# A gated MLP's down projection in a two-block fp32 kernel, from 88 direct block products a layer to 77 by Strassen's scheme

## The chip, the cores and the metric

The kernel runs on one core of a Trainium2 chip. The metric is the device time of one execution in microseconds (us). TensorE (PE, with its weight loads shown apart as PEld) multiplies, VectorE (DVE), ScalarE (ACT) and GpSimd (POOL) work on elements, and the queue of SyncE (SPq) issues nearly all DMA transfers.

## The reference, cut to what matters

A first block (an RWKV branch beside latent attention) is followed by two layers of a second block. Everything is fp32, the sequence has 256 tokens and the model width is 1024. Each of the two layers ends in this, with `D_FF` = 2816:

```python
def conv_gated_mlp(x, w_up, conv_w, conv_b, w_down):
    h = x @ w_up
    hp = jnp.pad(h, ((0, 0), (CONV_WIDTH - 1, 0), (0, 0)))
    acc = conv_b
    for i in range(CONV_WIDTH):
        acc = acc + conv_w[i] * hp[:, i:i + seq]
    gate, val = jnp.split(acc, 2, axis=-1)
    return (jax.nn.gelu(gate) * val) @ w_down
...
        h = h + conv_gated_mlp(xn, w_up[layer], conv_w[layer], conv_b[layer], w_down[layer])
```

The change is about the last product, (256 x 2816) by (2816 x 1024), and the addition of its result to `h`.

## The kernel before

Each engine has one instruction stream, written by hand, and the streams meet at semaphores. The residual `h` is `xc[:, t, :]`, 128 tokens in each of t = 0, 1.

**Up projection.** It runs in 22 blocks m of 128 channels. TensorE fills one PSUM bank for a block (gate and value halves side by side, line 1343). VectorE then goes through a loop over m (lines 2758 to 2777): `scaled_rows(m + 1)` drains the next block's bank (line 2749), four multiply-adds apply the convolution (2767), three operations prepare the GELU (2771 to 2775), and `gate_part(m - 1)` (2755, 2757) writes `actT[:, m - 1, :]` after ScalarE's tanh. After the loop comes `gate_part(21)`. `actT[:, k, :]` holds 128 channels by 256 tokens, and the semaphore `act_T` counts these blocks. ScalarE's share for a block (lines 1869 and 1863) waits for `act_T` of two blocks before.

**Banks.** A pool "short" of six banks and a pool "long" of two are handed out in turn by `turn(key)`. `filling`, `when_full`, `emptying` and `when_empty` name the semaphores of a bank's current use.

**Weights.** A ring of four 2 MB slots is filled by SyncE's queue in the order of use, two transfers to a slot. A slot is filled again when the tile in it is released. `w_down` comes in six tiles `("down", l, n)`, of four blocks of 128 rows each (two in the last one).

**Down projection.** For each of the 22 blocks k, TensorE runs four products (line 1362), one for each of the quarters (t, j), j being a half of the 1024 columns, and each adds into its own bank over all k. One such fp32 product of 128x128 by 128x512 is two matmul instructions with a weight load each in the trace. VectorE adds the four banks into `xc` (line 2791), in the order (0,0), (1,0), (0,1), (1,1).

**Work of the next layer in that stretch.** Between `gate_part(21)` of layer 0 and those additions, VectorE runs what layer 1's state-space part needs: `state_steps` (from line 2294), `state_inputs` (from 2329), `state_sums` (from 2364), `state_maps` (2383, 2386) and two `sine_angles` (2392, 2394). The last operation of `state_steps` releases GpSimd's `raw_angles` (line 2838), one multiplication of 128x2048. Layer 1 has no such work behind it.

**End.** SyncE waits for all four additions of layer 1 and stores the whole output (1 MB) in one transfer (line 2963).

Of the kernel before, what the change touches and what calls it, by code (L numbers as in the profile page):

```python
# [15 lines left out]
P = 128  # L16
# [20 lines left out]
UP_TILES = FB // PAIRS  # L37
DOWN_K = 4
DOWN_TILES = -(-FB // DOWN_K)
RING_1, RING_2 = 3, 4  # L40
SLOT = KD * 512
TWO_PI = 2.0 * math.pi
# [70 lines left out]
def weight_tiles(w):  # L113
# [54 lines left out]
SCORES = [(0, (0, 1, 2, 3))] * 2 + [(1, (0, 1))] * 2 + [(1, (2, 3))] * 2  # L168
BLOCK = 32

SEMAPHORES = """a_bar_sc act_T cc_zero first_consts hT_even hT_odd ssq_ctx angle angle_raw b_spread a_made bk_ch block_T bonus_in c0 c_masked cv_made c_silu c_tanh consts crow d_bias d_hat
 d_rstd d_var d_w decays derived dt_exp e_made ends g_tanh gelu_in gelu_tanh h0 hp_pads k_tok kk_rn kk_sq kkf
 lam_exp lam_sum lora lw_in k_rate maps_used m_bias mix_gmlp mix_rw mix_ssm mod_cols off_made off_step out_done p2_load pads
 params_1 params_2 q_tok qk_rot qk_rstd qk_sum qk_taken qk_turned qk_var r_ch r_grown rk_used rotated rotated_used rstd_1 rstd_f rstd_lat scale_a scanned row_inv
# [4 lines left out]
def build(nc, w, consts, out):  # L179
# [16 lines left out]
    with ExitStack() as ctx:  # L196
# [210 lines left out]
        hp = take_work(M0 + 16128, 2, 2, 258)  # L407
        cv = take_work(M0 + 17160, 2, 2, SEQ)
        ge = take_work(M0 + 18184, 2, 2, SEQ)
        assert H0 + 2304 <= NW - (RING_2 - RING_1) * SLOT  # L410

        def shift_dest(key):
# [22 lines left out]
        def _(pe):  # L435
# [672 lines left out]
            for l in range(DEPTH):  # L1108
# [39 lines left out]
                            ins = tr(b[:, (2 * j + c) * P:(2 * j + c + 1) * P], bexp[:, j, c].rearrange("p a b -> p (a b)"), ident)  # L1148
                    ins.then_inc(*filling(("bT", l)))
                if l:  # L1150
                    to_channels("xa", xc, lambda j: when_empty(("down", l - 1, 2 + j)), small_maps)
                else:
                    to_channels("xa", xs2, lambda j: (S["z_f"], 2 * j + 2), small_maps)

# [178 lines left out]
                for n in range(UP_TILES):  # L1333
# [15 lines left out]
                pe.wait_ge(*turn(("down", l, 0)))  # L1349
                pe.wait_ge(*turn(("down", l, 1)))  # L1350
                pe.wait_ge(*turn(("down", l, 2)))
                pe.wait_ge(*turn(("down", l, 3)))
                acc = [bank_of(("down", l, 0)), bank_of(("down", l, 1)), bank_of(("down", l, 2)), bank_of(("down", l, 3))]
                for n in range(DOWN_TILES):
                    rows = min(DOWN_K, FB - n * DOWN_K)
                    wt = weights(("down", l, n), rows, 1024)
                    for q in range(rows):
                        k = DOWN_K * n + q
                        pe.wait_ge(S["act_T"], FB * l + k + 1)
                        for j in range(2):  # L1360
                            for t in range(2):
                                ins = mm(acc[2 * t + j][:, :], actT[:, k, P * t:P * t + P], wt[:, q, 512 * j:512 * j + 512],  # L1362
                                         start=(k == 0), stop=(k == FB - 1))
                                if k == FB - 1:
                                    ins.then_inc(*filling(("down", l, 2 * t + j)))
                    if n < DOWN_TILES - 1:
                        weights_done(ins=ins)
                    else:
                        weights_done(("down", l, 3))


        @block.scalar
        def _(act):
# [347 lines left out]
            for l in range(DEPTH):  # L1721
# [23 lines left out]
                if l:  # L1745
                    state_times(l)
                    state_parameters(l)
                    for q in range(4):
                        if q == 2:
                            channels_even(l, "xa", "attn_g", 0)  # L1750
                        square_sum(2 * l, q, when_empty(("down", l - 1, 2 * (q % 2) + q // 2)))
                channels_even(l, "xa", "attn_g", 2)
                take_maps()
                if l:
# [123 lines left out]
        def _(vec):  # L1878
# [640 lines left out]
            for l in range(DEPTH):  # L2519
# [231 lines left out]
                def gate_part(m):  # L2751

                    vec.wait_ge(S["gelu_tanh"], FB * l + m + 1)
                    p = m % 2
                    STT(out=ge[:, p, 1, :], in0=ge[:, p, 1, :], scalar=1.0, in1=cv[:, p, 0, :], op0=ADD, op1=MUL).then_inc(S["vec_step"], 1)
                    vec.wait_ge(S["vec_step"], next(vec_steps))
                    STT(out=actT[:, m, :], in0=ge[:, p, 1, :], scalar=0.5, in1=cv[:, p, 1, :], op0=MUL, op1=MUL).then_inc(S["act_T"], 1)  # L2757
                scaled_rows(0)
# [20 lines left out]
                if l + 1 < DEPTH:  # L2779
                    state_steps(l + 1)  # L2780
                    state_inputs(l + 1)
                    state_sums(l + 1)
                    state_maps(l + 1)
                    sine_angles(l + 1, 0)
                    sine_angles(l + 1, 1)
                for q in (0, 2, 1, 3):
                    t, j = q // 2, q % 2
                    vec.wait_ge(*when_full(("down", l, q)))
                    b = bank_of(("down", l, q))
                    x = xc[:, t, 512 * j:512 * j + 512]  # L2790
                    TT(x, x, b[:, :], ADD).then_inc(*emptying(("down", l, q)))  # L2791
                    vec.wait_ge(*when_empty(("down", l, q)))


        @block.gpsimd
# [85 lines left out]
        def _(sp):  # L2881
# [77 lines left out]
                        dst = dst.rearrange("p (k n) -> p k n", k=shape[0])  # L2959
                    sp.dma_start(dst, src).then_inc(slot_full[slot_of[n]], 16)  # L2960
            for q in range(4):
                sp.wait_ge(*when_empty(("down", DEPTH - 1, q)))
            sp.dma_start(out.rearrange("a (t p) d -> p (a t) d", p=P), xc[:, 0:2, :]).then_inc(S["out_done"], 16)
            sp.wait_ge(S["out_done"], 16)
# [20 lines left out]
```

## Time and profile before

| | us |
|---|---|
| median of three runs | 1183.38 (1181.89 to 1184.08) |
| span of the profiled execution | 1187.4 |
| down projection in the chain, layer 0, layer 1 | 75.53, 75.55 |
| up projection in the chain, layer 1 | 145.04 |
| last addition, then the store until it has landed | 0.69, 4.0 |

For the profiled execution the profile gives the span, from its first instruction to its last, and no other time of its own; the span is 4.0 us above the median of the runs. Times in rows are counted from the start of that span. A row of a timeline is: start, duration from the first to the last of the merged instructions, engine, line, operation, out<-in, shape, count, and in brackets the idle time before it with what ended it. The start-to-start distance of two neighbouring rows is often shorter than the duration of the first, because an engine starts the next instruction while the last one drains.

### The profile page before, as it was taken

The numbers are of one execution on the slowest core, as the hardware profiler recorded it, in microseconds if no ns is written. First come the engines' busy times: TensorE is split into PE (matmuls) and PEld (weight loads), VectorE is DVE, ScalarE is ACT, GpSimd is POOL, SyncE is SP. The second block draws the span as 40 slices with busy tenths as digits, with TensorE's granted clock in tenths as the row PEclk, the third lists the DMA queues.
The fourth block names the chain that finished last, engine by engine and source line by source line (L and its number), as shares of the span: only waits on it lengthen the run. The fifth ranks groups of instructions, "written<-read, shape, count | busy, mean of one in ns | idle before, by whom it ended". The sixth has DMA issues, their size and how long they took to land.

```text
span 1187.4 us, 15600 instructions
## 1 busy us (share of the span) xinstructions
PE 1136.4 (96%) x6191; PEld 793.8 (67%) x6191; DVE 645.7 (54%) x1360; ACT 336.6 (28%) x786; POOL 111.0 (9%) x107
## 2 busy tenths in 40 slices
PE   4899999989979999999999999999999999999998
PEld 2444857767878696555478888644555488888543
DVE  3222315688879944898226656631798135666400
ACT  2212213775633504325121121200525112112100
POOL 0000101210120011261000000100351000000000
PEclk9799999999888977999999999999999999999999
DMA  9722332000004211832248443424522354454410
GB/s 357 275 71 72 128 142 76 1 1 1 2 1 125 83 37 36 290 135 71 71 141 258 142 142 147 172 106 143 181 101 71 108 176 142 144 166 172 157 35 36
DMA packets 96666, 140.06 MB, mean 118 GB/s; under 512 B 12207, under 2 KB 63058, under 8 KB 96466
## 3 DMA queue, kind: packets, MB, share of 16 engines
q1 hardware_dynamic: 96228, 138.94, 34.3%
q8 instruction: 49, 0.80, 0.3%
q14 instruction: 23, 0.19, 0.1%
q10 hardware_dynamic: 366, 0.13, 0.0%
HBM read 138.01 MB, written 1.05 MB: 117 GB/s over the span
## 4 chain that ended last, share of the span: by engine, by line
PE 75%; DVE 18%; ACT 2%; issue 2%; DMA 2%; SPq 0%; POOL 0%; DVEq 0%; ACTq 0%
PE bank L1343 26%; PE bank L1362 13%; PE bank L826 12%; PE bank L480 2%; PE bank L473 2%; PE bank L1171 2%; DMA ring<-in_ada_w 2%; DVE work L2617 2%; DVE work L2612 1%; DVE ring L2175 1%; PE bank L619 1%; PE bank L1102 1%; PE bank L1161 1%; PE bank L812 1%; DVE rot L2597 1%
## 5 line engine op out<-in xcount | busy, mean ns | idle before, releaser
L1343 PE MATMUL bank<-work,ring 128*128 128x256 f32 x1024 | 222.7, 379 | 0.0
L1343 PEld LDWEIGHTS bank<-work,ring 128*128 128x128 f32 x1024 | 194.2, 190 | 26.2
L826 PE MATMUL bank<-work,ring 128*128 128x256 f32 (+1 forms) x432 | 141.1, 485 | 2.4 <-ACT work L1413 2.4
L1362 PE MATMUL bank<-ring,work 128*128 128x512 f32 x288 | 124.3, 592 | 0.0
L826 PEld LDWEIGHTS bank<-work,ring 128*128 128x128 f32 x432 | 82.8, 195 | 56.0 <-issue 49.4
L1869 ACT ACTIVATE work<-work,prm 128x256 f32<-128x256 f32 x88 | 48.0, 592 | 250.5 <-DVE work L2757 224.0
L1362 PEld LDWEIGHTS bank<-ring,work 128*128 128x128 f32 x288 | 54.7, 190 | 68.0 <-issue 67.4
L2749 DVE TENSOR_TENSOR work<-bank,turned 128x512 f32<-128x512 f32 x44 | 30.4, 692 | 112.0 <-PE bank L1343 111.9
L1343 PE MATMUL bank<-work 128*128 128x256 f32 x384 | 83.9, 379 | 0.0
L1343 PEld LDWEIGHTS bank<-work 128*128 128x128 f32 x384 | 73.0, 190 | 9.9
L2767 DVE SCALAR_TENSOR_TENSOR work<-work,prm 128x256 f32<-128x256 f32 x176 | 77.1, 480 | 4.2 <-ACT work L1869 2.6
L2802 POOL TENSOR_TENSOR small<-small,con 128x8 f32<-128x8 f32 (+4 forms) x23 | 32.6, 1418 | 429.6 <-DVE small L1987 123.2
L1171 PE MATMUL bank<-ring,work 128*128 128x512 f32 (+1 forms) x192 | 71.7, 526 | 0.0
L2791 DVE TENSOR_TENSOR xc<-xc,bank 128x512 f32<-128x512 f32 x8 | 5.5, 688 | 108.9 <-PE bank L1362 108.9
L1171 PEld LDWEIGHTS bank<-ring,work 128*128 128x128 f32 x192 | 35.7, 190 | 31.8 <-issue 30.3
L1967 DVE SCALAR_TENSOR_TENSOR work<-work,prm 128x512 f32<-128x512 f32 x10 | 7.5, 752 | 56.4 <-ACT work L1436 56.4
L2736 DVE TENSOR_TENSOR xc<-xc,bank 128x512 f32<-128x512 f32 x8 | 5.5, 688 | 46.9 <-PE bank L480 46.9
L1742 ACT ACTIVATE work<-xc 128x512 f32<-128x512 f32 x12 | 7.5, 629 | 78.8 <-DVE xc L2791 58.7
L480 PE MATMUL bank<-ring,mixT 128*128 128x512 f32 x64 | 27.9, 594 | 2.0 <-ACT mixT L1853 2.0
L1779 ACT ACTIVATE work<-work,small 128x64 f32<-128x64 f32 x64 | 16.2, 335 | 44.9 <-DVE work L2599 44.9
L1171 PE MATMUL bank<-work 128*128 128x512 f32 x64 | 28.7, 596 | 0.0
L2838 POOL TENSOR_TENSOR work<-small,con 128x2048 f32<-128x2048 f32 x2 | 7.3, 3654 | 225.3 <-DVE small L2319 163.9
(454 smaller groups left out, 1772.4 us busy)
## 6 DMA issues: line engine op xcount, KB each, us to landing
ring<-in_w_up SPq DMA_DIRECT2D x32, 1024.0 KB, 7.7
ring<-in_w_in SPq DMA_DIRECT2D x24, 1024.0 KB, 7.7
ring<-in_w_down SPq DMA_DIRECT2D x16, 1024.0 KB, 5.9
ring<-in_ada_w SPq DMA_DIRECT2D x12, 1024.0 KB, 11.0
work<-in_w_up SPq DMA_DIRECT2D x12, 1024.0 KB, 7.7
ring<-in_w_out SPq DMA_DIRECT2D x10, 1024.0 KB, 6.2
work<-in_w_in SPq DMA_DIRECT2D x4, 1024.0 KB, 8.5
work<-in_w_down SPq DMA_DIRECT2D x4, 1024.0 KB, 5.8
```

The costliest lines, as they stand in the source:

```text
L473: mm(b[:, :], mixT[:, k, P * t:P * t + P], out_weights[j][:, k, :], start=(k == ks[0]), stop=False)
L480: ins = mm(b[:, :], mixT[:, k, P * t:P * t + P], out_weights[j][:, k, :], start=False, stop=(k == ks[-1]))
L826: ins = mm(b[0:rows, 0:toks], wt[:, k, off:off + rows], hT[:, k, 0:toks], start=(k == 0), stop=(k == KD - 1))
L1171: ins = mm(b[:, 0:cols], xnT[:, k, P * t:P * t + P], wt[:, k, off:off + cols], start=(k == 0), stop=(k == KD - 1))
L1343: ins = mm(b[:, SEQ * half:SEQ * half + SEQ], wt[:, KD * half + k, P * j:P * j + P], xnT[:, k, :], start=(k == 0), stop=(k == KD - 1))
L1362: ins = mm(acc[2 * t + j][:, :], actT[:, k, P * t:P * t + P], wt[:, q, 512 * j:512 * j + 512], start=(k == 0), stop=(k == FB - 1))
L1779: ins = A.activation(qkr[:, c, t, 64 * h:64 * h + 64], rot_a[:, h, :], ACT.Copy, scale=small[:, 296 + 8 * i + h:297 + 8 * i + h])
L1869: ins = A.activation(cv[:, m % 2, half, :], hp[:, m % 2, half, 2:SEQ + 2], ACT.Identity, scale=k2(l, "conv2", 1, FB * half + m), bias=k2(l ...
L2617: ins = V.tensor_tensor_scan(gs[:, s % 2, SEQ * c:SEQ * c + SEQ], small[:, 440 + s:441 + s].to_broadcast([P, SEQ]), xr[:, SEQ * c:SEQ * c ...
L2749: TT(hp[:, p, :, 2:SEQ + 2], bank_of(("up", l, m))[:, :].rearrange("p (a n) -> p a n", a=2), rep(scale_row, 2), MUL).then_inc(*emptying((" ...
L2767: ins = STT(out=cv[:, p, half, :], in0=hp[:, p, half, tap:tap + SEQ], scalar=k2(l, "conv01", 1, 44 * tap + FB * half + m), in1=cv[:, p, ha ...
L2802: return G.tensor_tensor(out_, in_, C("negpow", 1, rows).to_broadcast([rows, n]), POW)
```

## The change

The 22 blocks of 128 rows are taken in 11 pairs. A pair with left blocks a(k, t) (k = the block of the pair, t = the tokens) and right blocks b(k, j) gives four quarters of the output. These come out of seven products instead of eight, and each of the seven adds into a bank of its own over all pairs: product 5 in a "long" bank, the other six in all six "short" banks. Seven left operands are needed for a pair, of which five are sums or differences (`row_sums`, for two pairs at once, five instructions over 2x128 elements), and seven right operands, of which five are sums or differences (`column_sums`, one pair at a time, five instructions of 128x512). VectorE forms all of them. The column sums have two buffers, by p % 2, so those of pair p wait until pair p - 2 is used. At the end, twelve additions or subtractions replace the four, in the order of the products 5, 1, 4, 7, 2, 3, 6. The last two pairs run interleaved, two products of the same number one after the other.

In VectorE's stream, `row_sums(0)` to `row_sums(4)` come at the ends of blocks m = 4, 8, 12, 16, 20, `column_sums(0)` and `(1)` at the ends of blocks 18 and 19, `row_sums(5)` and `column_sums(2)` after the loop, and `column_sums(3)` to `(7)` each behind one part of the next layer's state work. The output leaves in four transfers of 256 KB, each after the last addition to its quarter.

```diff
+DOWN_ORDER = (5, 1, 4, 7, 2, 3, 6)
+DOWN_LAST = (7, 2, 3, 6)
...
+                def down_product(i, p, last):
+                    wt, q = down_w[p // 2], 2 * (p % 2)
+                    one, two = actT[:, 2 * p, 0:P], actT[:, 2 * p + 1, P:2 * P]
+                    left = {1: row_sum[:, 0, p, :], 2: row_sum[:, 1, p, :], 3: one, 4: two, 5: row_sum[:, 2, p, :], 6: row_sum[:, 3, p, :], 7: row_sum[:, 4, p, :]}[i]
+                    cs = col_sum[p % 2]
+                    right = {1: cs[0], 2: wt[:, q, 0:512], 3: cs[1], 4: cs[2], 5: wt[:, q + 1, 512:1024], 6: cs[3], 7: cs[4]}[i]
+                    return mm(bank_of(("down", l, i))[:, :], left, right, start=(p == 0), stop=last)
...
+                for p in range(DOWN_PAIRS - 2):
+                    if p % 2 == 0:
+                        down_weights(p // 2)
+                    pe.wait_ge(S["row_sums"], 6 * l + p // 2 + 1)
+                    for i in DOWN_ORDER:
+                        if p == 0:
+                            pe.wait_ge(*turn(("down", l, i), "long" if i == 5 else "short"))
+                        if i == 1:
+                            pe.wait_ge(S["column_sums"], DOWN_PAIRS * l + p + 1)
+                        ins = down_product(i, p, False)
...
+                    ins.then_inc(S["pair_used"], 1)
+                down_weights(DOWN_TILES - 1)
+                pe.wait_ge(S["row_sums"], 6 * l + 6)
+                for i in DOWN_ORDER:
+                    if i == 1:
+                        pe.wait_ge(S["column_sums"], DOWN_PAIRS * (l + 1))
+                    ins = down_product(i, DOWN_PAIRS - 2, False)
...
+                    ins = down_product(i, DOWN_PAIRS - 1, True)
+                    ins.then_inc(*filling(("down", l, i)))
...
+                def column_sums(p):
+                    n, q = index[("down", l, p // 2)], 2 * (p % 2)
+                    vec.wait_ge(slot_full[slot_of[n]], 32 * fills[n])
+                    if p >= 2:
+                        vec.wait_ge(S["pair_used"], (DOWN_PAIRS - 2) * l + p - 1)
...
+                    TT(cs[0], b11, b22, ADD)
+                    TT(cs[2], b21, b11, SUB)
+                    TT(cs[4], b21, b22, ADD)
+                    TT(cs[1], b12, b22, SUB)
+                    TT(cs[3], b11, b12, ADD).then_inc(S["column_sums"], 1)
...
                     if m:
                         gate_part(m - 1)
+                    if m and m % 4 == 0:
+                        row_sums(m // 4 - 1)
+                    if m in (18, 19):
+                        column_sums(m - 18)
                 gate_part(FB - 1)
+                row_sums(5)
+                column_sums(2)
...
+                added(5, (0, 0, SUB), (0, 1, ADD))
+                added(1, (0, 0, ADD), (1, 1, ADD))
+                added(4, (0, 0, ADD), (1, 0, ADD))
+                added(7, None, (0, 0, ADD))
+                added(2, (1, 1, SUB), (1, 0, ADD))
+                added(3, (1, 1, ADD), (0, 1, ADD))
+                added(6, None, (1, 1, ADD))
```

`row_sums(n)` waits for `act_T` of its four blocks and then runs five instructions. An addition of `added` waits for the one before it. The left blocks `one` and `two` and the right blocks `wt[...]` are read where they lie, so products 2 and 5 need no column sum. The readers of `xc` behind layer 0 (transposes on TensorE, squares on ScalarE) now wait for the last addition to each quarter, `DOWN_LAST`.

## Rows read from the trace of the kernel before

**Rows 1.** The page's first line.

```profile
span 1187.4 us, 15600 instructions
```

**Rows 2.** The chain that ended last: start, us, what.

```profile
753.84 75.53 PE bank L1362 x176
...
1106.56 75.55 PE bank L1362 x176
...
1182.19 0.69 DVE xc L2791
```

**Rows 3.** The down products' line: ns min/median/max, first and last start.

```profile
L1362 PEld LDWEIGHTS bank<-ring,work x288: 190/190/190, 753.5 to 1181.1; 128*128 128x128 f32 x144
```

**Rows 4.** VectorE's timeline, layer 1, up blocks 18, 20 and 21.

```profile
1092.78 0.69 DVE L2749 TENSOR_TENSOR work<-bank,turned 128x512 f32<-128x512 f32 x1 [2.47 <-PE bank L1343]
...
1096.00 0.42 DVE L2775 TENSOR_TENSOR work<-work 128x256 f32<-128x256 f32 x1
1096.34 0.42 DVE L2755 SCALAR_TENSOR_TENSOR work<-work 128x256 f32<-128x256 f32 x1
1096.79 0.42 DVE L2757 SCALAR_TENSOR_TENSOR work<-work 128x256 f32<-128x256 f32 x1
...
1106.59 0.69 DVE L2749 TENSOR_TENSOR work<-bank,turned 128x512 f32<-128x512 f32 x1 [2.47 <-PE bank L1343]
...
1112.33 1.80 DVE L2767 SCALAR_TENSOR_TENSOR work<-work,prm 128x256 f32<-128x256 f32 x4 [1.30 <-ACT work L1869]
...
1116.54 0.42 DVE L2757 SCALAR_TENSOR_TENSOR work<-work 128x256 f32<-128x256 f32 x1
```

**Rows 5.** SyncE's queue: issues of down weights, layer 1.

```profile
1065.15 14.69 SPq L2960 DMA_DIRECT2D ring<-in_w_down  x4
```

**Rows 6.** VectorE's timeline, layer 0, the next layer's state work.

```profile
764.17 0.23 DVE L2294 TENSOR_SCALAR small<-small,con 128x8 f32<-128x8 f32 x1
...
769.10 1.93 DVE L2329 TENSOR_TENSOR small<-small 128x8 f32<-128x8 f32 x1 [1.79 <-ACT small L1675]
...
773.91 0.29 DVE L2364 TENSOR_TENSOR work<-small,work 128x128 f32<-128x128 f32 x1
...
775.87 1.39 DVE L2383 TENSOR_SCALAR work<-work,con 128x64 f32<-128x64 f32 x8
777.17 0.69 DVE L2386 TENSOR_TENSOR work<-work,con 128x512 f32<-128x512 f32 x1
777.77 0.69 DVE L2392 TENSOR_SCALAR work<-work 128x1024 f32<-128x1024 f32 x1
```

**Rows 7.** GpSimd's timeline in the same stretch.

```profile
767.39 3.62 POOL L2838 TENSOR_TENSOR work<-small,con 128x2048 f32<-128x2048 f32 x1 [163.86 <-DVE small L2319]
```

**Rows 8.** The timeline of all engines, layer 1's scans.

```profile
882.33 1.27 POOL L2867 TENSOR_TENSOR work<-work 128x512 f32<-128x512 f32 x1
882.37 1.78 DVE L2612 TENSOR_TENSOR work<-work 128x512 f32<-128x512 f32 x1
```

**Rows 9.** Windows: busy us of each engine, granted TensorE clock, DMA share, GB/s.

```profile
259.00:263.00 4.00, 1.08 (x7) 0.62 (x6) 3.80 (x9) 1.33 (x5) 0.00 (x0) 1.00 0.00 0
263.00:267.00 4.00, 4.00 (x27) 2.93 (x26) 3.65 (x13) 2.59 (x8) 0.00 (x0) 1.00 0.02 4
...
340.00:343.50 3.50, 0.10 (x1) 0.00 (x0) 3.38 (x5) 2.69 (x6) 1.93 (x3) 1.00 0.00 0
...
346.00:353.70 7.70, 7.70 (x50) 7.36 (x51) 2.67 (x5) 1.08 (x2) 0.72 (x2) 0.50 0.00 0
```

**Rows 10.** TensorE's timeline: the starts that ended those two stalls.

```profile
262.76 0.63 PE L568 MATMUL bank<-con,xc 128*128 128x128 f32 x4 [2.92 <-ACT xc L1630]
...
345.99 0.45 PE L661 MATMUL bank<-work,ring 128*128 128x64 f32 x1 [5.89 <-DVE ring L2048]
```

**Rows 11.** DMA issues: KB each, median us to landing.

```profile
out<-xc SPq DMA_DIRECT2D x1, 1024.0 KB, 4.0
...
work<-in_gmlp_w_s SPq DMA_DIRECT2D x2, 256.0 KB, 2.9
```

More of the change, by code:

```diff
@@ L409, in build @@
         ge = take_work(M0 + 18184, 2, 2, SEQ)
+        row_sum = take_work(M0 + 2048, 5, DOWN_PAIRS, P)
+        col_sum = ([mixT[:, 2 * i:2 * i + 2, :].rearrange("p a b -> p (a b)") for i in range(4)] + [rot_flat],
+                   [take_work(a, 512) for a in (M0 + 9088, M0 + 9600, G0 + 3072, G0 + 3584, G0 + 4096)])
         assert H0 + 2304 <= NW - (RING_2 - RING_1) * SLOT
@@ L1150, in _ @@
                 if l:
-                    to_channels("xa", xc, lambda j: when_empty(("down", l - 1, 2 + j)), small_maps)
+                    to_channels("xa", xc, lambda j: when_empty(("down", l - 1, DOWN_LAST[2 * j + 1])), small_maps)
                 else:
@@ L1348, in _ @@
                     weights_done(("up", l, m))
[L1349 to L1366, printed above, removed]
+                down_w = {}
@@ new lines, in down_weights @@
+                def down_weights(n):
+                    down_w[n] = weights(("down", l, n), min(DOWN_K, FB - n * DOWN_K), 1024)
+                for p in range(DOWN_PAIRS - 2):
[8 more added lines that the diff above has]
+                        ins = down_product(i, p, False)
+                        if i == 2 and p % 2:
+                            weights_done(ins=ins)
+                    ins.then_inc(S["pair_used"], 1)
@@ L1372, in _ @@
+                weights_done(("down", l, 2))
         @block.scalar
@@ L1750, in _ @@
                             channels_even(l, "xa", "attn_g", 0)
-                        square_sum(2 * l, q, when_empty(("down", l - 1, 2 * (q % 2) + q // 2)))
+                        square_sum(2 * l, q, when_empty(("down", l - 1, DOWN_LAST[q])))
                 channels_even(l, "xa", "attn_g", 2)
@@ L2757, in gate_part, with row_sums @@
                     STT(out=actT[:, m, :], in0=ge[:, p, 1, :], scalar=0.5, in1=cv[:, p, 1, :], op0=MUL, op1=MUL).then_inc(S["act_T"], 1)
+                def row_sums(n):
+                    first, last = 2 * n, min(2 * n + 2, DOWN_PAIRS)
+                    vec.wait_ge(S["act_T"], FB * l + 2 * last)
+                    a = actT[:, 2 * first:2 * last, :].rearrange("p (n k) (t c) -> p n k t c", k=2, t=2)
+                    a11, a12, a21, a22 = a[:, :, 0, 0], a[:, :, 1, 0], a[:, :, 0, 1], a[:, :, 1, 1]
+                    TT(row_sum[:, 0, first:last, :], a11, a22, ADD)
+                    TT(row_sum[:, 1, first:last, :], a21, a22, ADD)
+                    TT(row_sum[:, 2, first:last, :], a11, a12, ADD)
+                    TT(row_sum[:, 3, first:last, :], a21, a11, SUB)
+                    TT(row_sum[:, 4, first:last, :], a12, a22, SUB).then_inc(S["row_sums"], 1)
+                def column_sums(p):
[3 more added lines that the diff above has]
+                        vec.wait_ge(S["pair_used"], (DOWN_PAIRS - 2) * l + p - 1)
+                    wt = slot(n)[:, 1024 * q:1024 * q + 2048].rearrange("p (k j c) -> p k j c", k=2, j=2)
+                    b11, b12, b21, b22 = wt[:, 0, 0], wt[:, 0, 1], wt[:, 1, 0], wt[:, 1, 1]
+                    cs = col_sum[p % 2]
+                    TT(cs[0], b11, b22, ADD)
[3 more added lines that the diff above has]
+                    TT(cs[3], b11, b12, ADD).then_inc(S["column_sums"], 1)
                 scaled_rows(0)
@@ L2777, in _, with add_product, added @@
                         gate_part(m - 1)
+                    if m and m % 4 == 0:
+                        row_sums(m // 4 - 1)
+                    if m in (18, 19):
+                        column_sums(m - 18)
                 gate_part(FB - 1)
-                if l + 1 < DEPTH:
+                row_sums(5)
+                column_sums(2)
+                more = l + 1 < DEPTH
+                if more:
                     state_steps(l + 1)
+                column_sums(3)
+                if more:
                     state_inputs(l + 1)
+                column_sums(4)
+                if more:
                     state_sums(l + 1)
+                column_sums(5)
+                if more:
                     state_maps(l + 1)
+                column_sums(6)
+                if more:
                     sine_angles(l + 1, 0)
+                column_sums(7)
+                if more:
                     sine_angles(l + 1, 1)
[L2786 to L2789, printed above, removed]
+                for p in range(8, DOWN_PAIRS):
+                    column_sums(p)
+                def add_product(i, t, j, op):
                     x = xc[:, t, 512 * j:512 * j + 512]
-                    TT(x, x, b[:, :], ADD).then_inc(*emptying(("down", l, q)))
-                    vec.wait_ge(*when_empty(("down", l, q)))
+                    return TT(x, x, bank_of(("down", l, i))[:, :], op)
+                def added(i, one, two):
+                    vec.wait_ge(*when_full(("down", l, i)))
+                    if one:
+                        add_product(i, *one).then_inc(S["vec_step"], 1)
+                        vec.wait_ge(S["vec_step"], next(vec_steps))
+                    add_product(i, *two).then_inc(*emptying(("down", l, i)))
+                    vec.wait_ge(*when_empty(("down", l, i)))
+                added(5, (0, 0, SUB), (0, 1, ADD))
[5 more added lines that the diff above has]
+                added(6, None, (1, 1, ADD))
         @block.gpsimd
```

17 lines of the change are left out of this document (9 added, 8 removed).

## The prediction, made before the changed kernel was run

> **What bounds the kernel now.** I read the chain of waits first, since a saving counts only where it shortens that chain. In both layers the down projection is one unbroken piece of TensorE work, 75.53 and 75.55 us [rows 2], and in layer 1 only one addition and the store stand behind it. So TensorE is the bound here and a product less is time less. A layer has 88 products, each two of the 176 matmuls of that piece: 75.55 / 88 = 0.859 us a product. Then VectorE's timeline, since it gets new work: in the up projection it works 4.4 of every 6.9 us and then waits for TensorE (the bracket of 2.47 us [rows 4]); in the down projection it is free but for layer 0's state work [rows 6]. The question is whether that slack lies where the sums are needed.
>
> **What is removed.** 11 products a layer: 77 x 0.859 = 66.1 us against 75.55, so 9.4 us a layer, 18.9 in all, if TensorE never waits.
>
> **Prices of the sums.** An independent 128x512 addition in SBUF starts 0.60 us before the next instruction and lasts 0.69 (777.17 to 777.77 [rows 6]). So `column_sums` is 5 x 0.60 = 3.0 us of VectorE's time, with its signal 4 x 0.60 + 0.69 = 3.1 us after its start. At 128x256 the distance is 0.34 (1096.00 to 1096.34 [rows 4]), so `row_sums` is 5 x 0.34 = 1.7, with 0.1 for its wait on the last `act_T`. At 128x128 the row lasts 0.29 [rows 6]; by the 0.08 that two neighbours overlap, the distance is 0.21 and `row_sums(5)` 1.05. The upper bound is a start only after the end, as for dependent neighbours (0.45 for 128x256 [rows 4], so 0.73 at 512). I take the lower figure, because the five instructions don't depend on each other.
>
> **VectorE's walk into the down projection.** Let 0 be the start of the down piece in the chain (1106.56 in layer 1). The `row_sums` of blocks 4 to 16 take 1.8 us of a slack of 2.47: free. Block 18 begins at -13.78 and its body takes 4.35 (1092.78 to 1096.79, and 0.34 [rows 4]). Its weight tile was issued 41 us ahead [rows 5], so `column_sums(0)` doesn't wait: 3.0, done at -6.4. That is already later than the -6.9 at which block 19 wants to begin. Block 19 with `column_sums(1)`: 7.35, to +0.9. Block 20: 4.35 and `row_sums(4)` 1.8, to +7.1. Block 21 has no bank to drain; in the trace it takes 1112.33 to 1116.96 with both last gate parts [rows 4], so 4.6: +11.7. `row_sums(5)`: +12.8. `column_sums(2)`: signal at +15.9. The drain of bank 21 falls at about +1.6, ahead of product 6 of pair 0, which takes that bank at +5.2, so no bank is waited for.
>
> **Stall 1, both layers.** A pair takes 7 x 0.859 = 6.01 us. Pairs 0 and 1 have their sums, so TensorE has run them and product 5 of pair 2 at 2 x 6.01 + 0.86 = +12.9. Product 1 then waits until 15.9, and with a signal and a weight load that wasn't run ahead (0.19 [rows 3]) starts at 16.15. **3.3 us lost.** The wait is ahead of product 1, so everything of the pair but product 5 is queued behind it.
>
> **After that, layer 1.** The sums of pair p may start when pair p - 2 is used and are needed 6.01 + 0.86 us later; they take 3.3 with the signals. No stall up to pair 9.
>
> **Stall 2, both layers: the last two pairs.** They run interleaved, so product 1 of pair 9 comes after two products 5, and it waits for the sums of pair 10. Those share a buffer with pair 8 and start when its last product is done (0.2 after it on the array, a matmul being longer than its distance to the next). 0.2 + 3.1 + 0.25 = 3.55, less 2 x 0.86: **1.8 us lost** in each layer, on a VectorE that was idle before.
>
> **Layer 0: the state work between the sums.** `column_sums(2)` frees VectorE at 15.8. `state_steps` takes 3.1 (764.17 to its release of GpSimd just ahead of 767.39 [rows 6, 7]): 18.9. Then GpSimd multiplies for 3.6 us. The trace shows what a VectorE addition with two SBUF operands does meanwhile: 1.93 for eight elements, ended with GpSimd's instruction, and 1.78 in place of 0.69 for one of 128x512 that began behind a GpSimd one [rows 6, 8]. The port is taken for a whole instruction, and the other waits. `SBUF — State Buffer` of the Trainium skill, section "SBUF: two separate sides", calls this an exclusive lock taken by whoever starts first; the trace agrees, by the 1.78 us. Either GpSimd gets in after the first sum of pair 3 (signal at 25.7), or after the fifth (signal at 22.0, and `state_inputs` waits until 25.6). Both ways `state_inputs` (2.9, from 771.03 to 773.91 [rows 6]) ends near 28.6 and the sums of pair 4 near 31.7. Product 1 of pair 4 starts at 32.0; without any stall it would at 4 x 6.01 + 0.86 = 24.9. So **7.1 us are lost by pair 4**, the 3.3 of stall 1 among them. `state_sums` (773.91 to 775.87, 2.0), `state_maps` (1.9, to 777.77) and the sine angles (two of 1.9, by the same timeline) with 3.1 of sums each are under 6.01, so VectorE catches up, and it stays hidden. Cover is thin there: a part over 2.9 us would show.
>
> **The ends.** Twelve additions replace four. They come two to a product of number i, 2 x 0.73 against 1.72 us of two products, so they keep up; the last one is alone, 0.69 after the last matmul, as before [rows 2]. The readers behind layer 0 find the other quarters done earlier, and this one at the same distance: nothing. Store: 1 MB landed 4.0 us after its issue, a 256 KB transfer in 2.9 [rows 11], though a load. Quarters one to three leave while TensorE or VectorE works. Bounds: 0 (a fixed cost fills the 4.0) and 2.0; I take 1.4, a little over 4.0 - 2.9, because a load's 2.9 shares its queue with others.
>
> **The clock.** Until now TensorE was never idle in this piece. Does a stall of 3.3 us lower it to 1.2 from 2.4 GHz? After a stall of 2.92 the granted clock stayed at 1.00; in one of 5.89 us it fell 3.5 us after the engine stopped, and 7.7 us of work then ran at 0.50 [rows 9, 10]. The stalls here (3.0 to 3.8 us) lie between. Bounds: nothing, and half of 7.7 = 3.9 us a stall; that row's work was sparse, this one is dense. I take 1.5 us for the whole run, one short fall. `TensorE: Matmul & The Clock Gate` of the Trainium skill, section "Why this matters for your kernels", speaks against this change, since it wants no idle gap over about 3 us between bursts; by it every stall 1 would cost, by the 2.92 row none would. No row shows a dense stream with such a gap.
>
> **Sum.** Layer 0: 9.4 - 7.1 - 1.8 = +0.5. Layer 1: 9.4 - 3.3 - 1.8 = +4.3. Store +1.4, clock -1.5. Gain 4.7 us, some 12 of 18.9 given back to waits. The walk is made in the profiled execution, whose span is 1187.4 [rows 1]; the median is 4.0 lower, or 0.3%, which changes no term. 1183.4 - 4.7 = **1178.7 us**.
>
> **Rivals.**
> 1. *VectorE keeps up.* The stalls are nearly gone: 18.9 + 1.4 = 20, so 1163. For it: VectorE is idle for 45 us of each down piece. Against it: the 29.6 us of listed work between -13.8 and +12.9, where only 26.7 fit. Chance 0.08. A middle case, where layer 0's state work hides but stall 1 stays, gives 18.9 - 2 x 5.1 + 1.4 = 10, so 1173: 0.10.
> 2. *The sums cost 0.73 each* (slower side of the price). Column sums are 3.65, row sums 2.2. The same walk gives a signal for pair 2 at 18.7, stall 1 of 6, stall 2 of 2.4, and 10.5 by pair 4 in layer 0: 21.3 lost of 18.9, with the store 1.0 slower, 1184.4. It decides from about 0.70 a sum. Against it: 777.17 to 777.77. Chance 0.08.
> 3. *The clock falls and stays down, slower than before.* If each stall of 3 us or more (one in layer 1, two in layer 0) brings 7.7 us at half clock, it costs 3 x 3.9 = 11.6 and not 1.5: 1183.4 - 4.8 - 1.4 + 11.6 = 1188.8. It decides from 6.2 us of clock loss. For it: the fall 3.5 us into the one long stall. Against it: 2.92 without one, and work that is dense on both sides. By the page's sentence this would be the outcome. Chance 0.12.
>
> The forecast keeps 0.62, between 1176 and 1182.5. A measurement of this kernel tells about 0.2%, 1181.0 and 1185.7, from no change. Faster: the forecast's 0.55 below 1181.0, and 0.18 of rival 1: 0.73. Same: the forecast's upper 0.07, and most of rival 2: 0.14. Slower: 0.13. The range for 8 in 10 takes in the middle case and rival 2: 1172 to 1185.
>
> **What would show it.** TensorE's matmuls of the down line, in the profile of the changed kernel: 77 products a layer, at the old distance. In the table of waits, TensorE on VectorE's column sums: two long waits in layer 1 (about 3.1 and 1.6), three or four in layer 0, 12 to 14 us in all. VectorE's timeline: `column_sums(2)` ends 15.9 us after TensorE's first down product. GpSimd's 128x2048 lies inside or right behind the sums of pair 3. The pieces: 75.0 and 71.2 us, longer by what the clock takes. The windows behind each stall show a granted clock of 1.00, or 0.50. The prediction is wrong if a column sum takes under 2.6 or over 3.5 us, if the clock stays down for more than some 6 us, or if another wait (a bank, a weight tile) appears among the first three pairs.

## The result, and the profile after

The changed kernel took 1177.43 us (median of 20 executions, 1171.11 to 1189.57) against 1184.4 (20 executions, 1178.09 to 1192.37) for the kernel before on the same chips. The ratio is 0.9938, its 95% interval 0.9918 to 0.9959, which is 7.3 us less (4.9 to 9.7); the two medians are 7.0 apart. The execution of 1189.57 us is a slow one and is left out of the ratio. The prediction was 1178.7, or 4.7 less than its 1183.4. The profiled execution took 1176.57 us with a span of 1174.8.

The page's first line, and the down products in the line's own view (ns min/median/max, first and last start):

```profile
span 1174.8 us, 15721 instructions
```

```profile
L1364 PE MATMUL bank<-work x116: 592/592/697, 755.1 to 1170.1; 128*128 128x512 f32 x116
...
L1364 PE MATMUL bank<-mixT,work x96: 592/592/1222, 749.1 to 1170.9; 128*128 128x512 f32 x96
...
L1364 PE MATMUL bank<-ring,work x72: 592/592/1001, 748.2 to 1167.5; 128*128 128x512 f32 x72
...
L1364 PE MATMUL bank<-rot,work x24: 592/592/1061, 750.8 to 1165.8; 128*128 128x512 f32 x24
```

These are 308 matmuls, 2 x 77 products of two each, in place of 352. The chain that ended last (start, us, what) no longer has the down projection as one piece [rows 2]; each layer's is broken where a column sum ended the wait:

```profile
767.90 4.02 DVE work L2802
773.78 35.53 PE bank L1364 x82
812.56 10.57 PE bank L1364 x24
...
1116.23 41.48 PE bank L1364 x96
1160.96 10.58 PE bank L1364 x24
```

TensorE's timeline shows the same from the array's side. The first row of each layer is the start of the down projection, the brackets are its waits, the last row its last product:

```profile
748.21 1.02 PE L1364 MATMUL bank<-ring,work 128*128 128x512 f32 x2
...
764.30 3.78 PE L1364 MATMUL bank<-mixT,work 128*128 128x512 f32 x4 [3.05 <-DVE mixT L2805]
...
773.78 2.84 PE L1364 MATMUL bank<-work 128*128 128x512 f32 x6 [0.19 <-DVE work L2805]
...
779.89 1.94 PE L1364 MATMUL bank<-mixT,work 128*128 128x512 f32 x4
...
812.56 1.12 PE L1364 MATMUL bank<-work 128*128 128x512 f32 x2 [1.54 <-DVE mixT L2805]
...
822.11 1.02 PE L1364 MATMUL bank<-mixT,work 128*128 128x512 f32 x2
...
1100.15 1.02 PE L1364 MATMUL bank<-ring,work 128*128 128x512 f32 x2
...
1116.23 1.98 PE L1364 MATMUL bank<-mixT,work 128*128 128x512 f32 x4 [3.04 <-DVE mixT L2805]
...
1160.96 1.12 PE L1364 MATMUL bank<-work 128*128 128x512 f32 x2 [1.55 <-DVE mixT L2805]
...
1170.50 1.02 PE L1364 MATMUL bank<-mixT,work 128*128 128x512 f32 x2
```

VectorE's timeline and GpSimd's row, from which come the sums' prices, the blocked sum in layer 0, and the last addition:

```profile
763.56 0.69 DVE L2805 TENSOR_TENSOR mixT<-ring 128x512 f32<-128x512 f32 x1
...
767.22 0.69 DVE L2801 TENSOR_TENSOR work<-ring 128x512 f32<-128x512 f32 x1
767.82 4.10 DVE L2802 TENSOR_TENSOR work<-ring 128x512 f32<-128x512 f32 x1
...
773.05 0.68 DVE L2805 TENSOR_TENSOR work<-ring 128x512 f32<-128x512 f32 x1
...
1112.06 0.29 DVE L2787 TENSOR_TENSOR work<-work 128x128 f32<-128x128 f32 x1
...
1113.08 0.68 DVE L2801 TENSOR_TENSOR mixT<-ring 128x512 f32<-128x512 f32 x1
...
1115.49 0.69 DVE L2805 TENSOR_TENSOR mixT<-ring 128x512 f32<-128x512 f32 x1
...
1171.63 0.69 DVE L2856 TENSOR_TENSOR xc<-xc,bank 128x512 f32<-128x512 f32 x1 [0.31 <-PE bank L1364]
```

```profile
767.38 3.99 POOL L2917 TENSOR_TENSOR work<-small,con 128x2048 f32<-128x2048 f32 x1 [169.32 <-DVE small L2342]
```

The store among the DMA issues (KB each, median us to landing), which answers to [rows 11]:

```profile
out<-xc SPq DMA_DIRECT2D x4, 256.0 KB, 2.0
```

**Where the time went.** The spans differ by 12.6 us, but that isn't all the change's. In this profile layer 0's down projection begins at 748.2, in that of before at 753.7, both counted from a first matmul; in the seven experiments on the changed kernel that start lies anywhere from 743.0 to 753.2, though nothing ahead of the down projection's sums differs, and at 748.1 in the kernel before with another store. I count that stretch as chance. Between the two down projections both profiles take the same 277.19 us (829.37 to 1106.56 before, 823.13 to 1100.32 after). What is left is the change's own:

| piece, us | before | after | gained | predicted |
|---|---|---|---|---|
| down projection, layer 0 (748.38 to 823.13) | 75.53 | 74.75 | 0.8 | 0.5 |
| down projection, layer 1 (1100.32 to 1171.52) | 75.55 | 71.20 | 4.35 | 4.3 |
| last addition's start to the end of the span | 5.2 | 3.2 | 2.0 | 1.4 |
| clock, for the whole run (a fall in layer 0 cost nothing, see below) | | | 0 | -1.5 |
| sum | | | 7.2 | 4.7 |

The pieces are counted 0.17 us behind the first matmul, as the chain of before does. The sum of 7.2 agrees with the 7.3 of the timed runs.

### The profile page after: what moved, and what is told of

Same layout as the page of the kernel before. It is cut to its first block, busy times and chain, and to the rows that moved or that the text cites. A ratio compares the mean times of both kernels' runs of the same rounds, so it can differ in the third digit from the quotient of the medians.

```text
span 1174.8 us, 15721 instructions
## 1 busy us (share of the span) xinstructions
PE 1114.0 (95%) x6147; PEld 777.2 (66%) x6147; DVE 744.5 (63%) x1546; ACT 336.8 (29%) x786; POOL 111.4 (9%) x107
## 3 DMA queue, kind: packets, MB, share of 16 engines
HBM read 138.01 MB, written 1.05 MB: 118 GB/s over the span
## 4 chain that ended last, share of the span: by engine, by line
PE 69%; DVE 24%; issue 3%; ACT 2%; DMA 2%; SPq 0%; POOL 0%; DVEq 0%; ACTq 0%
PE bank L1349 24%; PE bank L832 12%; PE bank L1364 8%; PE bank L486 2%; PE bank L479 2%; PE bank L1177 2%; DMA ring<-in_ada_w 2%; DVE work L2640 2%; DVE work L2635 1%; DVE ring L2198 1%; PE bank L625 1%; PE bank L1108 1%; PE bank L1167 1%; DVE work L2815 1%; DVE rot L2620 1%
## 5 line engine op out<-in xcount | busy, mean ns | idle before, releaser
L1349 PEld LDWEIGHTS bank<-work 128*128 128x128 f32 x384 | 73.0, 190 | 9.9
L1364 PE MATMUL bank<-work 128*128 128x512 f32 x116 | 54.3, 595 | 3.3 <-DVE mixT L2805 3.1
L1177 PEld LDWEIGHTS bank<-ring,work 128*128 128x128 f32 x192 | 35.7, 190 | 31.8 <-issue 30.3
L1364 PE MATMUL bank<-mixT,work 128*128 128x512 f32 x96 | 47.8, 615 | 6.1 <-DVE mixT L2805 6.1
L1364 PEld LDWEIGHTS bank<-work 128*128 128x128 f32 x116 | 21.8, 190 | 32.1 <-issue 26.3
L1364 PEld LDWEIGHTS bank<-mixT,work 128*128 128x128 f32 x96 | 18.5, 195 | 30.7 <-issue 22.3
L1364 PE MATMUL bank<-ring,work 128*128 128x512 f32 x72 | 36.5, 598 | 0.0
L2759 DVE TENSOR_TENSOR xc<-xc,bank 128x512 f32<-128x512 f32 x8 | 5.5, 687 | 46.9 <-PE bank L486 46.9
```

What stands on the lines that cost most here:

```text
L1177: ins = mm(b[:, 0:cols], xnT[:, k, P * t:P * t + P], wt[:, k, off:off + cols], start=(k == 0), stop=(k == KD - 1))
L1349: ins = mm(b[:, SEQ * half:SEQ * half + SEQ], wt[:, KD * half + k, P * j:P * j + P], xnT[:, k, :], start=(k == 0), stop=(k == KD - 1))
L1364: return mm(bank_of(("down", l, i))[:, :], left, right, start=(p == 0), stop=last)
```

## The experiments

My theory is the prediction's walk: the 11 products are really saved, 9.4 us a layer, and what is lost again is lost at (a) stall 1, because `column_sums(2)` stands behind too much VectorE work, (b) stall 2, because pair 10 shares a buffer with pair 8, and (c) in layer 0, GpSimd's multiplication between the sums of pair 3. The rival is that the array doesn't run sums at the old rate, or that waits taken away come back as others (VectorE too slow, a clock fall behind each stall). "First to last start" below is the time from TensorE's first to its last matmul row in a down projection: 73.90 and 70.35 us in the changed kernel. In the version without waits it is 65.24. Ratios are to the kernel before on the same chip: 1185.28 us for the first four experiments, 1184.42 for the others. A single execution has no ratio, and its time says little, since the changed kernel's own executions lie between 1171 and 1190; there the trace carries the reading.

### One store

```diff
                 sp.wait_ge(*when_empty(("down", DEPTH - 1, DOWN_LAST[q])))
-                sp.dma_start(out[0, P * t:P * t + P, 512 * j:512 * j + 512], xc[:, t, 512 * j:512 * j + 512]).then_inc(S["out_done"], 16)
-            sp.wait_ge(S["out_done"], 64)
+            sp.dma_start(out.rearrange("a (t p) d -> p (a t) d", p=P), xc[:, 0:2, :]).then_inc(S["out_done"], 16)
+            sp.wait_ge(S["out_done"], 16)
```

> The changed kernel with its store put back into one transfer of 1 MB after the last addition; nothing else differs. My theory: of the 7.1 us that the profile shows as gained beside the clock's chance falls, 2.0 lie behind the last addition (5.2 us from its start to the end of the span before, 3.2 after). So the tail returns to 5.2 us, the two down pieces stay at 74.6 and 71.3, and the time is 2.0 us above the changed kernel, about 1179.5. Rival: the quarters only hide behind each other and what shortened the tail is something else; then the tail stays near 3.2 us.

1179.7 us, ratio 0.9953 (0.9927 to 0.998), against 0.9938 (0.9918 to 0.9959) with the quarters: the timed runs alone don't tell the two apart. In the profile, the last addition and the span's end (1175.7) are 5.25 us apart, as before the change:

```profile
1170.45 0.69 DVE L2856 TENSOR_TENSOR xc<-xc,bank 128x512 f32<-128x512 f32 x1 [0.31 <-PE bank L1364]
```

So the quarters are worth 2.1 us there (5.25 against 3.17). Layer 0's first to last start was 73.89, as in the changed kernel; layer 1's first to last start was 72.06 in place of 70.35. A window right behind layer 1's stall 1 (busy us by engine, granted clock, DMA share, GB/s) shows why:

```profile
1113.60:1117.00 3.40, 3.40 (x5) 1.36 (x6) 2.71 (x5) 0.00 (x0) 0.00 (x0) 0.52 0.26 107
```

The clock was at its lower level for 3.4 us of work, which costs half of that, 1.7.

### Pair 2's sums one block earlier

```diff
-                    if m and m % 4 == 0:
+                    if m and m % 4 == 0 and m < 20:
-                    if m in (18, 19):
+                    if m in (18, 19, 20):
...
+                column_sums(3)
+                row_sums(4)
                 row_sums(5)
-                column_sums(2)
...
-                column_sums(3)
```

> Order of VectorE's work alone: the sums of pair 2 move to the end of up block 20, and the row sums that stood there (of pairs 8 and 9) and of pair 10, which nobody needs for another 40 us, go behind the sums of pair 3. My theory (VectorE is late with pair 2 by its own queue): signal of pair 2 at +9.3 us after the down piece's start in place of 15.9, needed at 12.9, so stall 1 is gone: layer 1's piece falls from 71.3 to 68.2. In layer 0 the state work and GpSimd's 4 us are the next to be late: pair 4 starts its product 1 at about +30.0 in place of 31.5, the piece falls by 1.5. Time -4.6 us against the changed kernel, about 1173. Rival 1: TensorE waits at that place for something else (a bank, a tile); then the stall keeps its 3 us. Rival 2: the stall's cost is mainly a lowered clock; then more than 3.3 us come back in layer 1.

1175.17 us, ratio 0.9914 (0.9888 to 0.994). In layer 1 first to last start is 67.05: 3.30 less, which is what the prediction charged for stall 1; the bracket of 3.04 shows less than its removal gives back. In layer 0 it is 76.13, 2.2 more. The expectation had placed the sums of pair 4 wrongly: in this kernel `state_steps` and `state_inputs` both stand ahead of them, and TensorE waits there once, and long:

```profile
785.60 3.43 PE L1364 MATMUL bank<-mixT,work 128*128 128x512 f32 x4 [7.37 <-DVE mixT L2805]
```

That is the lateness of layer 0 moved, not removed. The clock has a part in it too: it was at its lower level from 781.7 to 788.6, and 3.0 us of that were work, so 1.5 of the 2.2 us are the clock's and 0.7 the longer wait's.

### A third buffer for the column sums

```diff
+                   [take_work(a, 512) for a in (M0, M0 + 512, M0 + 1024, M0 + 1536, H0 + 512)])
...
-                    cs = col_sum[p % 2]
+                    cs = col_sum[p % 3]
...
-                    if p >= 2:
-                        vec.wait_ge(S["pair_used"], (DOWN_PAIRS - 2) * l + p - 1)
+                    if p >= 3:
+                        vec.wait_ge(S["pair_used"], (DOWN_PAIRS - 2) * l + p - 2)
```

Four of the five new tiles lie where the up projection's input was, which is free by then.

> A third buffer for the column sums (the sums of pair p wait for pair p - 3 in place of p - 2), all work in the same order. My theory: stall 2, ahead of product 1 of pair 9, is the wait of pair 10's sums for pair 8's buffer, so it goes in both layers, 1.6 us each; stall 1 is VectorE's queue and not a buffer, so it stays at 3.1, and layer 0 stays 6.6 us late by pair 4. Layer 1's piece 71.3 to 69.7, layer 0's 74.6 to 73.0, time -3.2 us, about 1174. Rival (the buffers are what is late everywhere): stall 1 goes too, and the pieces fall to about 66.5 us.

1176.34 us, ratio 0.9921 (0.9888 to 0.9955). Apart from one of 0.19 us in layer 0, the only waits left on column sums are the two stalls 1 (us in all, times, longest):

```profile
PE bank L1365 <- DVE work L2806: 6.1, 2, 3.1
```

Stall 2 is gone in both layers. Layer 0: 72.09, 1.8 less. Layer 1: 70.24, or 1.8 less and 1.7 more, since the clock was down behind its stall:

```profile
1118.80:1122.10 3.30, 3.30 (x5) 1.33 (x4) 3.30 (x7) 0.00 (x0) 0.00 (x0) 0.51 0.06 24
```

### Both, and the state work placed later

The third buffer and the earlier sums of pair 2 are as above. Behind the loop over m the order is new; this is the code as it then stands. `more` is true in layer 0 alone.

```python
                gate_part(FB - 1)
                more = l + 1 < DEPTH
                column_sums(3)
                column_sums(4)
                if more:
                    state_steps(l + 1)
                column_sums(5)
                row_sums(4)
                row_sums(5)
                column_sums(6)
                if more:
                    state_inputs(l + 1)
                column_sums(7)
                if more:
                    state_sums(l + 1)
                    state_maps(l + 1)
                column_sums(8)
                if more:
                    sine_angles(l + 1, 0)
                column_sums(9)
                column_sums(10)
                if more:
                    sine_angles(l + 1, 1)
```

> Both together, and layer 0's state work spread so that no part stands ahead of a sum that is due: order after the up loop is the sums of pairs 3 and 4, state_steps, pair 5, the late row sums, pair 6, state_inputs, pair 7, state_sums and state_maps, pair 8, one half of the angles, pairs 9 and 10, the other half. My theory, that all 12 us given back are waits on VectorE's order and on two buffers: no wait on column sums over 0.3 us in either layer, both pieces 66.1 to 66.6 us, and a time 13 us below the changed kernel, about 1164, or 0.983 of the kernel before. Rival: TensorE pays for reading operands that VectorE has just written (a longer distance between products than 0.859 us), or GpSimd's port still makes it late in layer 0; then layer 1's piece stays over 67.5, or layer 0's stays over 68.

1165.78 us (1162.36 to 1173.2), ratio 0.984 (0.9799 to 0.9881): 19.0 us (14.1 to 23.8) below the kernel before, and the fastest of all. Its chain:

```profile
749.73 66.09 PE bank L1365 x154
...
1093.01 66.11 PE bank L1365 x154
1159.21 0.69 DVE xc L2857
```

Each down projection is one unbroken piece again, of 66.1 us: 77 x 0.859 to the tenth. The whole 9.4 us a layer is there, and 2.0 of the store: 20.9 by the pieces, within the interval of the timed runs. The clock stayed at its upper level through both pieces. GpSimd still blocks a column sum for four microseconds, and nobody waits for it now:

```profile
772.26 4.10 DVE L2803 TENSOR_TENSOR work<-work 128x512 f32<-128x512 f32 x1
```

```profile
771.82 4.00 POOL L2918 TENSOR_TENSOR work<-small,con 128x2048 f32<-128x2048 f32 x1 [172.41 <-DVE small L2343]
```

### The kernel before, with the store in quarters

```diff
-            for q in range(4):
+            for q in (0, 2, 1, 3):
+                t, j = q // 2, q % 2
                 sp.wait_ge(*when_empty(("down", DEPTH - 1, q)))
-            sp.dma_start(out.rearrange("a (t p) d -> p (a t) d", p=P), xc[:, 0:2, :]).then_inc(S["out_done"], 16)
-            sp.wait_ge(S["out_done"], 16)
+                sp.dma_start(out[0, P * t:P * t + P, 512 * j:512 * j + 512], xc[:, t, 512 * j:512 * j + 512]).then_inc(S["out_done"], 16)
+            sp.wait_ge(S["out_done"], 64)
```

> The kernel before with one part of the change alone: its four additions as they were, each quarter stored by its own transfer as soon as it is added. The additions end only 0.86 us apart there, so all four transfers of 256 KB leave in the last 3.3 us. My theory: what shortens the tail is that only the last quarter's transfer stands behind the last addition; the last one then shares the DMA engines with the quarter ahead of it, so from the start of the last addition to the end of the span 3.5 to 4.0 us in place of 5.2 (the changed kernel has 3.2 with its quarters 1.7 us apart). Gain 1.2 to 1.7 us. Rival: the spacing by the seven products is what pays, and four transfers close together take as long as the one; then the tail stays at 5.0 to 5.2.

1182.76 us, ratio 0.9981 (0.996 to 1.0002). The timing alone doesn't settle it; the profile does. From the last addition to the span's end (1180.2) it is 3.6 us, against 5.2 [rows 1, 2]:

```profile
1176.56 0.69 DVE L2791 TENSOR_TENSOR xc<-xc,bank 128x512 f32<-128x512 f32 x1 [0.17 <-PE bank L1362]
```

So the smaller last transfer gives 1.6 us without Strassen's scheme, and 0.5 more with it (3.64 against 3.17).

### GpSimd's multiplication cut to eight columns

```diff
+                if l:
+                    G.tensor_tensor(ang[:, 0, 0:8], small[:, 448:456], C("time", 8), MUL).then_inc(S["angle_raw"], 1)
+                    return
```

> The changed kernel with layer 1's angle multiplication on GpSimd cut from 128x2048 to 128x8, so the angles of layer 1 are left out. In the changed kernel's profile the second sum of pair 3 took 4.10 us in place of 0.68 while GpSimd held the port, so pair 3's signal came at +25.3. Now it comes at +22.0 and pair 4's at 28.0 (31.3 before). How much TensorE gains depends on its clock: in the changed kernel's profile it ran at half clock for 6.8 us around the end of stall 1, which made pair 2 last 9.3 us and hid behind the same late signal. From first to last down matmul of layer 0 (73.9): 70.6 if the clock stays up, 72.3 if it is down for 3.4 us, 73.6 if for 6.8 us. Rival (the port is no part of it, the state work alone is late): 73.9 stays whatever the clock does.

1175.15 us, one execution, of a kernel that leaves out the angles of layer 1. The sums of pair 3 now run at their own length beside a GpSimd instruction of 0.58 us:

```profile
768.25 0.69 DVE L2802 TENSOR_TENSOR work<-ring 128x512 f32<-128x512 f32 x1
```

Layer 0's first to last start is 72.05, layer 1's the same 70.35 as in the changed kernel. The clock was down in layer 0 from 765.5 to 768.9, which costs 1.7: without GpSimd, layer 0 is layer 1 plus a clock fall. Of the 3.6 us by which the changed kernel's layer 0 is longer than its layer 1, GpSimd's instruction and the clock are all.

### A longer stall 1 in layer 1

```diff
-                def column_sums(p):
+                def column_sums(p, signal=True):
...
+                    ins = TT(cs[3], b11, b12, ADD)
+                    if signal:
+                        ins.then_inc(S["column_sums"], 1)
...
+                if l:
+                    column_sums(2, False)
                 column_sums(2)
```

The same five sums are formed once more, and the first time without their signal.

> The changed kernel with the five sums of pair 2 formed twice in layer 1, which makes stall 1 there 3.1 us longer, 6.1 in all. Three profiles with a stall of 3.05 us at that place showed no fall of the clock once, and a fall for 3.4 us twice, at a cost of 1.7 us. Theory (a stall of 3 us stands at the edge, one of 6 is clearly over): the granted clock falls for 6.8 us or more, a part of it inside the stall; from first to last down matmul of layer 1 70.35 + 3.1 + 1.7 to 3.4 = 75.2 to 76.9 us. Rival (the falls are chance and don't go with the stall's length): 73.5, or 75.2 at most.

1186.79 us, one execution. The wait is twice as long, and the clock goes down inside it and stays down for 6.2 us of work:

```profile
1123.39 3.78 PE L1364 MATMUL bank<-mixT,work 128*128 128x512 f32 x4 [6.17 <-DVE mixT L2805]
```

```profile
1119.40:1123.30 3.90, 0.00 (x0) 0.00 (x0) 3.87 (x8) 0.00 (x0) 0.00 (x0) 0.50 0.53 220
1123.40:1129.60 6.20, 6.20 (x8) 2.58 (x9) 2.94 (x5) 0.00 (x0) 0.00 (x0) 0.50 0.00 0
```

First to last start in layer 1 is 76.55, 6.2 more than 70.35: 3.1 are the longer wait, 3.1 half of those 6.2 us of work.

### The last two pairs one after the other

```diff
-                        pe.wait_ge(S["column_sums"], DOWN_PAIRS * (l + 1))
+                        pe.wait_ge(S["column_sums"], DOWN_PAIRS * (l + 1) - 1)
                     ins = down_product(i, DOWN_PAIRS - 2, False)
...
+                for i in DOWN_ORDER:
+                    if i == 1:
+                        pe.wait_ge(S["column_sums"], DOWN_PAIRS * (l + 1))
                     ins = down_product(i, DOWN_PAIRS - 1, True)
```

> The changed kernel with its last two pairs run one after the other, not interleaved. My theory of stall 2 (pair 10's sums wait for pair 8's buffer, and product 1 of pair 9 stands behind them): it goes, and TensorE ends its layer 1 piece 1.8 us earlier (first to last product start 70.35 to 68.5). But the seven products then end 0.86 us apart, and eleven of the twelve additions at 0.73 us each don't fit: the last addition ends about 3.9 us after TensorE's last matmul in place of 0.73. Tail +3.1, so layer 1 and the store together are 1.3 us slower than in the changed kernel. Rival: stall 2 stays, because something other than the buffer holds pair 10.

1175.18 us, one execution. Stall 2 is gone with two buffers too: layer 1's first to last start is 71.55, of which 3.1 is a clock fall (1110.1 to 1117.0), so 68.45 in place of 70.35; layer 0's is 72.06 in place of 73.90. The additions now come one product apart, so VectorE falls behind TensorE. From the last product's start to the end of the last addition it is 4.5 us in place of 1.8:

```profile
1165.49 1.88 PE L1364 MATMUL bank<-mixT,work 128*128 128x512 f32 x4
```

```profile
1162.25 8.62 DVE L2859 TENSOR_TENSOR xc<-xc,bank 128x512 f32<-128x512 f32 x12 [3.70 <-PE bank L1364]
```

So 1.9 us of wait are exchanged for 2.7 at the end: the interleaving was no loss in layer 1, and the third buffer is the better cure.

## Why the prediction was right

**Removed work: right.** 0.859 us a product and 77 of them give 66.1; the version without waits measures 66.09 and 66.11.

**Prices of the sums: right.** Five column sums take from 1113.08 to 1116.18, 3.10 (predicted 3.1); `row_sums(5)` from 1112.06 to 1113.08, 1.02 (1.05). The lower of my two figures held, because the additions start 0.60 apart while each lasts 0.69: an independent one starts before the one ahead of it has ended. Rival 2 falls.

**The walk: right.** The signal of `column_sums(2)` came 15.9 us after the start of the down piece (1115.49 + 0.69 less 1100.32), as predicted. Stall 1 was predicted at 3.3 and its removal gave 3.30; stall 2 at 1.8, and its removal gave 1.8 in layer 0 (73.90 to 72.09), where the clock was down for 6.8 us in both kernels.

**Layer 0: the loss right, its make-up incomplete.** GpSimd got in behind the first sum of pair 3 (the row of 4.10 us), the later of my two cases: signal at +25.4 (predicted 25.7). Pair 4 began at +31.5 (predicted 32.0). But I had TensorE waiting for pairs 3 and 4. The trace shows a wait of 0.19 and none, because the clock fell at the end of stall 1 (the first of the windows below: 0.54 over 6.6 us) and pair 2 took 9.3 us in place of 6.0. So two causes lie side by side there, the clock and the sums of pair 3, and only the longer counts. Taking GpSimd away alone shows 1.7 of the clock; with GpSimd the fall costs nothing. "One store" shows it from the other side: there the clock was down for 3.4 us in place of 6.8, the wait ahead of pair 3 was 1.51 in place of 0.19, and first to last start was 73.89, the same as here.

```profile
770.90 2.84 PE L1364 MATMUL bank<-work 128*128 128x512 f32 x6 [1.51 <-DVE work L2805]
```

In the table of waits, TensorE on column sums comes to 9.4 us (the row below and one of 0.2), not the 12 to 14 that I gave as the sign, for the same reason: 3.1 us of what I counted as waiting were slow work.

```profile
PE bank L1364 <- DVE mixT L2805: 9.2, 4, 3.1
```

**The ends: mis-sized.** I took 1.4 for the store and it is 2.0, the upper bound that I had named. The measured landing of a 256 KB store is 2.0 us, not the 2.9 of a load of that size [rows 11].

**The clock: near in size, but too few falls reckoned with.** A stall of 3.05 us in layer 1, with dense work on both sides, occurs in five profiles. In two (the changed kernel, GpSimd cut) the clock didn't fall; the changed kernel's windows, first right behind stall 1 of layer 0, then in and behind that of layer 1:

```profile
764.30:770.90 6.60, 6.60 (x9) 2.76 (x10) 6.12 (x17) 1.71 (x3) 3.52 (x1) 0.54 0.19 78
...
1113.20:1116.10 2.90, 0.00 (x0) 0.00 (x0) 2.90 (x6) 0.00 (x0) 0.00 (x0) 1.00 1.04 425
1116.30:1122.30 6.00, 6.00 (x14) 2.69 (x15) 3.43 (x6) 0.00 (x0) 0.00 (x0) 1.00 0.19 76
```

In two (one store, third buffer) it was down for 3.4 us, costing 1.7 each, and in one (in turn) for 6.8, costing 3.1. The mean of the five is 1.3; I had taken 1.5 for the whole run. In layer 0 it fell around the end of stall 1 in all six profiles that have that stall, for 3.4 or 6.8 us, and not at all in the version without stalls. I had reckoned with one short fall in all. That the falls of layer 0 cost nothing, because the sums of pair 3 came later still, is not in the prediction, so it is luck that the clock term came out near. The prediction also named more than some 6 us at the lower clock as a sign of being wrong. This sign appeared, 6.8 us in layer 0, and was badly chosen, since it asked for the length of a fall and not for what waits behind it. Rival 3 supposed 3.9 for each of three stalls, and falls at that size. `TensorE: Matmul & The Clock Gate` of the Trainium skill, section "Why this matters for your kernels", warns of idle gaps over about 3 us; these stalls are at that edge, and the trace agrees with the warning, not with a certain loss: 9 falls in 11 such stalls, at 0 to 3.1 us of time each.

**Sum.** The terms gave 4.7, the pieces 7.2, the timed runs 7.3 (4.9 to 9.7). Of the 2.5 between terms and pieces, 1.5 is the clock, which this profile doesn't show, 0.6 the store, and 0.3 layer 0. The forecast of 4.7 lies just below the interval of the timed runs, so these terms were too small by more than noise. What the clock costs in the timed runs wasn't measured: they have one mean clock each and no trace. The prediction's "some 12 of 18.9 given back to waits" isn't the sum of its own losses (7.1 + 1.8 + 3.3 + 1.8 = 14.0); measured are 13.8, by 18.9 less 0.8 and 4.35. Rival 1 was wrong for this kernel, and its figure of 1163 is what the kernel comes to once the sums are ordered by when TensorE needs them: 1165.8.

## What to carry to other kernels

When work moves from the bound engine to an idle one, walk the idle engine's stream in order against the moment at which each result is needed; its busy share (VectorE worked 63 of 75 us in layer 0's piece and 48 of 71 in layer 1's) says nothing of that. The remedy is order and buffers, not speed: one block of lead, a third buffer and state work placed behind the sums that are due turned a gain of 7 us into one of 19 with the same instructions. Compare the pieces that the change touches, not the spans of two profiles: here 5.5 of 12.6 us came from ahead of it.

## What was not expected of the hardware

In all six profiles in which GpSimd's 128x2048 multiplication came due during the sums of pair 3 or 5, GpSimd got between two independent VectorE additions that stood ready one behind the other. In the changed kernel it started at 767.38 during the first, and the second took 4.10 us in place of 0.69, to the end of GpSimd's (3.99, against 3.62 where VectorE was not adding [rows 7]). A fall of the clock behind a stall was not the same from one profile to the next (none, 3.4 or 6.8 us in the same place), so a single profile doesn't tell what such a stall costs. The bracket of a wait understated its cost by 0.25 us at both stalls.
